# Seven-product input projections in two more blocks, and a modulation product shared by three engines during output projections

## The reference

```python
def modulation(cond, w, b):
    m = jax.nn.silu(cond) @ w + b
    return m.reshape(cond.shape[0], 1, N_MOD, D_MODEL)

def modulate_in(x, g_pre, mod, j):
    return rmsnorm(x, g_pre) * (1.0 + mod[:, :, 3 * j + 1]) + mod[:, :, 3 * j]

def gated_residual(x, out, g_post, mod, j, weight):
    return x + weight * mod[:, :, 3 * j + 2] * rmsnorm(out, g_post)

def swiglu(h, w13, w2):
    a, g = jnp.split(h @ w13, 2, axis=-1)
    return (jax.nn.silu(g) * a) @ w2
```

## Time and profile before

| | us |
|---|---|
| median of 3 runs | 2538.57 (2536.57 to 2541.32) |
| the profiled execution's own time | 2541.83 |
| its span, first to last instruction | 2540.0 |
| PE busy | 2476.5 (97%) |
| DVE busy | 1581.6 (62%) |
| ACT busy | 764.9 (30%) |
| POOL busy | 224.6 (9%) |

### The profile page before, as it was taken

One profiled execution on the slowest core, in us unless ns is written; L12 is line 12 of the kernel. 1 busy time (PEld: TensorE's weight loads), 2 busy tenths in 40 slices (PEclk: granted clock), 3 DMA queues, 4 the chain that ended last, 5 costly groups with the idle time before them and its releaser, 6 DMA issues. The chain is left out here.

```text
span 2540.0 us, 40285 instructions
## 1 busy us (share of the span) xinstructions
PE 2476.5 (97%) x15180; PEld 2295.7 (90%) x15180; DVE 1581.6 (62%) x2779; ACT 764.9 (30%) x1418; POOL 224.6 (9%) x299
## 2 busy tenths in 40 slices
PE   6999999999998899999999999999999999999998
PEld 5998999799888789989988998899799979989997
DVE  4887588734554678738875885233454458845864
ACT  4111111333444441111124211111331153523432
POOL 0000000201114210000002000000110011201211
PEclk9999999999999999999999999999999999999999
DMA  6554445333223335434551553222312223323332
GB/s 242 160 141 133 133 149 167 107 77 81 48 56 88 88 107 149 134 100 141 149 170 55 150 153 99 80 74 87 96 59 75 87 79 117 83 71 99 88 113 103
DMA packets 385035, 278.64 MB, mean 110 GB/s; under 512 B 39414, under 2 KB 354550, under 8 KB 383894
## 3 DMA queue, kind: packets, MB, share of 16 engines
q1 hardware_dynamic: 384918, 277.06, 36.4%
HBM read 270.04 MB, written 6.94 MB: 109 GB/s over the span
## 5 line engine op out<-in xcount | busy, mean ns | idle before, releaser
L1879 DVE TENSOR_TENSOR w_lo<-w_raw,w_hi 128x1024 fp32r<-128x1024 f32 (+1 forms) x363 | 354.5, 979 | 501.2 <-ACT w_hi L1303 496.8
L1303 ACT ACTIVATE w_hi<-w_raw 128x1024 fp32r<-128x1024 f32 (+1 forms) x363 | 309.2, 854 | 832.4 <-PE psum L921 425.3
L921 PE MATMUL psum<-hT_hi,w_hi 128*128 128x320 f32 x2432 | 554.8, 309 | 4.0 <-DVE w_lo L1879 3.3
L921 PE MATMUL psum<-hT_lo,w_hi 128*128 128x320 f32 x2432 | 554.1, 309 | 0.0
L921 PE MATMUL psum<-hT_hi,w_lo 128*128 128x320 f32 x2432 | 553.8, 309 | 0.0
L921 PEld LDWEIGHTS psum<-hT_hi,w_hi 128*128 128x128 f32 x2432 | 406.3, 188 | 5.7 <-DVE w_lo L1879 2.8
L921 PEld LDWEIGHTS psum<-hT_lo,w_hi 128*128 128x128 f32 x2432 | 406.8, 188 | 0.0
L921 PEld LDWEIGHTS psum<-hT_hi,w_lo 128*128 128x128 f32 x2432 | 406.6, 188 | 0.0
L1848 DVE SCALAR_TENSOR_TENSOR mod_acc<-ada_raw,cond_silu,mod_acc 128x256 f32<-128x256 f32 x896 | 365.4, 479 | 0.0
L848 PE MATMUL psum<-w_hi,act_hi 128*128 128x512 f32 x800 | 318.1, 398 | 4.6 <-DVE w_lo L1879 4.5
L849 PE MATMUL psum<-w_lo,act_hi 128*128 128x512 f32 x800 | 316.3, 395 | 0.0
(11 more groups left out here) (281 smaller groups left out, 3548.1 us busy)
## 6 DMA issues: line engine op xcount, KB each, us to landing
w_raw<-in_ffn_w_dram SPq DMA_DIRECT2D x156, 512.0 KB, 4.1
ada_raw<-in_ada_w_dram SPq DMA_DIRECT2D x128, 512.0 KB, 3.6
w_raw<-in_ffn_w_dram SPq DMA_DIRECT2D x148, 256.0 KB, 2.7
w_raw<-in_ab_w_in_dram SPq DMA_DIRECT2D x28, 512.0 KB, 4.1
w_raw<-in_sc_w_in_dram SPq DMA_DIRECT2D x24, 512.0 KB, 4.0
w_raw_next<-in_ffn_w_dram SPq DMA_DIRECT2D x20, 512.0 KB, 5.2
ada_first<-in_ada_w_dram SPq DMA_DIRECT2D x4, 2048.0 KB, 19.0
held_raw<-in_ffn_w_dram SPq DMA_DIRECT2D x28, 256.0 KB, 3.7
```

Of the source, the lines that this page charges most:

```text
L921: last = mm(IN[p][0:width, h, 0:HT], a, b[:, k, h * HT:(h + 1) * HT], start=(k == 0 and a is hi and b is hT_hi), stop=(k == KD - 1 and a i ...
L1303: A(dst, src, ACT.Copy).then_inc(w_hi_ok, 1)
L1879: V.tensor_tensor(d_, a, b.bitcast(F32), ALU.subtract).then_inc(w_lo_ok, 1)
```

## The change

The third and fourth block take the seven-product form as well, with three plain pairs in the first half. The jobs of these blocks go (`JOBS` keeps block 0). Layer 1's modulation is now made in nine *sums* of 1024 columns (`MODS`): three in the first output stage of block 2 and one in its second, the same in block 3, and the ninth in the first output stage of block 5. A sum has 8 *steps*, one per slice k. A step loads a tile `ada_tile` of 128 x 1024 (512 KB, three slots). VectorE multiplies and adds the first 576 columns for both conditions, as before; of the other 448 ScalarE makes the two scaled copies (one to `mod_scaled`, one over the tile), and GpSimd adds them to its accumulators. After 8 steps TensorE sums over the partitions with a column of ones (`pick`), 8 matmuls of 288 or 224 columns on four column groups (`modulation`). VectorE adds the bias (`modulation_rows`) and SyncE stores the rows. The steps of a first output stage stand at units 1 to 17 (24 steps; block 5's eight at the same pace, at units 1 to 5), those of a second at units 2 to 9 (8 steps). The output stages use other PSUM banks, and the x rows that were loaded back evenly in the second output stage are, but for the first, now loaded after its last weight.

Core of the diff. `load_mods` runs on SyncE behind the load of unit u's weight, `modulation` on TensorE behind output unit u, `scale_step` on ScalarE, the first `add_step` on GpSimd and the second on VectorE:

```diff
-PLAIN = {5: (3, 0)}
+PLAIN = {2: (3, 0), 3: (3, 0), 5: (3, 0)}
...
-JOBS = {0: (0, 2 * D, (HF, HF), (3, 3)), 2: (1, 0, (HF, HF), (1, 1)), 3: (1, 6 * D, (HF, 0), (1, 0))}
+JOBS = {0: (0, 2 * D, (HF, HF), (3, 3))}
+MODS = {2: ([(1, 0), (1, D), (1, 2 * D)], [(1, 3 * D)]), 3: ([(1, 4 * D), (1, 5 * D), (1, 6 * D)], [(1, 7 * D)]), 5: ([(1, 8 * D)], [])}
+GROUPS = (288, 288, 224, 224)
+ON_DVE, MODC = 576, 1024
+SUM_AT = lambda ph, z: STEP_AT(ph["half"], len(ph["mods"]))[8 * z + 7] + (2 if ph["half"] == 0 else 0)
+STEP_AT = lambda half, n: [1 + j * 17 // 24 for j in range(8 * n)] if not half else [2 + j for j in range(8 * n)]
...
+            def load_mods(ph, u):
+                n = len(ph["mods"])
+                at_u = STEP_AT(ph["half"], n)
+                for j in range(8 * n):
+                    if (2 if j < 3 else at_u[j - 3] + 3) != u:
+                        continue
+                    g = 8 * ph["mb"] + j
+                    if j == 0:
+                        load_bias_rows(ph, 0)
+                        sp.wait_ge(pe_prod, SEVEN * ph["g1"])
+                    if j >= 3:
+                        sp.wait_ge(ada_used[0], USED(g - 3))
+                        sp.wait_ge(ada_used[1], USED(g - 3))
+                    layer, col = ph["mods"][j // 8]
+                    slot, count = TILE(g)
+                    src = ada_w[layer].rearrange("(p k) n -> p k n", k=KD)[:, j % 8, col:col + MODC]
+                    dma(ada_tile[ph["half"]][slot][:], src).then_inc(ada_landed[slot], 16)
...
+            def modulation(ph, u):
+                    pe.wait_ge(ada_used[0], USED(8 * b + 7))
+                    pe.wait_ge(ada_used[1], USED(8 * b + 7))
...
+                    for cd in range(2):
+                        for i in range(4):
+                            acc, c = (ACC_D(ph, z), G_AT[i]) if i < 2 else (ACC_P(ph, z), G_AT[i] - ON_DVE)
+                            last = mm(PS[32 * i:32 * i + 2, bank, 0:GROUPS[i]], pick[:, 1 - cd:3 - cd], acc[:, cd, c:c + GROUPS[i]], start=(cd == 0), stop=(cd == 1))
+                    last.then_inc(mod_mm, 1)
...
+            def scale_step(ph, j):
+                act.wait_ge(ada_landed[slot], count)
...
+                tile = ada_tile[h][slot][:, ON_DVE:MODC]
...
+                if k > 2:
+                    act.wait_ge(ada_used[1], USED(g - 2))
+                A(scaled[h][:, k % 2, :], tile, ACT.Copy, scale=csil[:, 0, k:k + 1])
+                A(tile, tile, ACT.Copy, scale=csil[:, 1, k:k + 1]).then_inc(mod_scaled, 1)
...
+            def add_step(ph, j):
...
+                pool.wait_ge(mod_scaled, g + 1)
+                pool.wait_ge(ada_used[1], USED(g - 1))
+                for cd, src in enumerate((scaled[h][:, k % 2, :], ada_tile[h][TILE(g)[0]][:, ON_DVE:MODC])):
+                    acc = ACC_P(ph, j // 8)[:, cd, :]
+                    pool.tensor_tensor(acc, acc, src, ALU.add).then_inc(ada_used[1], 1)
...
+            def add_step(ph, j):
+                dve.wait_ge(ada_landed[slot], count)
...
+                    if k == 0:
+                        V.tensor_scalar(acc, w, col, None, ALU.mult).then_inc(ada_used[0], 1)
+                    else:
+                        V.scalar_tensor_tensor(acc, w, col, acc, ALU.mult, ALU.add).then_inc(ada_used[0], 1)
```

More of the change, by code:

```diff
@@ L1031, in out_phase @@
                     last.then_inc(pe_unit, 1)
+                    if seven(ph):
+                        modulation(ph, u)
                 if not held:
@@ L1410, in out_splits @@
                             split_held(s, ph, i)
+                    if seven(ph):
+                        for j, at_u in enumerate(STEP_AT(ph["half"], len(ph["mods"]))):
+                            if at_u == u:
+                                scale_step(ph, j)
                 if final:
@@ L1756, in _ @@
                             pool.tensor_tensor(S2[:], S1[:], A11(g), ALU.subtract).then_inc(ws_ok, 1)
+                        for j in range(8 * len(ph["mods"])):
+                            add_step(ph, j)
                 if kind == "sc":
@@ L2034, in out_phase @@
                             split_held(s, ph, i)
+                    if seven(ph):
+                        for z in range(len(ph["mods"])):
+                            if min(SUM_AT(ph, z) + 3, len(units) - 1) == u:
+                                modulation_rows(ph, z)
+                        for j, at_u in enumerate(STEP_AT(ph["half"], len(ph["mods"]))):
+                            if at_u == u:
+                                add_step(ph, j)
                     z, r = divmod(u - 1 - LATE[ph["half"]] if late else u, 3)
-                    sooner = 2 if late and not final else 0
+                    sooner = 2 if (late or seven(ph)) and not final else 0
                     if sooner and u == K + 1:
```

209 lines of the change are left out of this document (172 added, 37 removed).

## The result

The changed kernel takes **2586.85 us**, the median of four runs (2584.41 to 2592.79), against 2538.94 for the kernel before (four runs now, one more than in the table ahead of the prediction): a ratio of **1.019**, 95% interval 1.017 to 1.021, so 48 us slower. The forecast was 2553, the range 2487 to 2582. The direction was right, the loss more than three times as large as forecast, and the time lies outside the range. Repeated runs of one kernel lie up to 10 us apart, so a difference of a few us against a kernel that ran once is not told from none.

What follows compares the result with a forecast made beforehand. TensorE, busy 97% of the span, was taken to bound the kernel. Terms -62.6 - 1 + 52.2 + 17.8 + 8.4 = +14.8 us on the profiled 2541.8 gave 2556.6, so a median of 2553 us; range 2487 to 2582.

Steps and rivals of the forecast that it cites:

- Part 1 and 2: Blocks three and four: the seven-product form saves 62.6 us; taking jobs out of the input stages saves 1 us.
- Part 3: The nine sums over partitions on TensorE, 8 small fp32 matmuls each: 1.1 us per sum.
- Part 4, the price of a turn: First output stages: VectorE and GpSimd take turns, so one addition and one VectorE step together cost 1.63 us.
- GpSimd's end: First output stage: GpSimd's chain of additions ends at 93.8 us, 88.8 plus 5 for tiles that land late.
- Part 4, the step that failed: First output stage: unit 18's split comes at 89.3 us, 4.5 before GpSimd's end; stage ends at 104.4, +26.1 each.
- evacuations on the path: Copies of finished banks out of PSUM delaying TensorE: +8, allowed only within the forecast's own range.
- its case's own range: Spread of the forecast's main case, which had chance 0.68: 2530 to 2573 us.
- Part 5 and 6: Eight steps in each second output stage, +8.9 each or +17.8; ninth sum in the sixth block's first output stage, +8.4.
- rival 2: VectorE and GpSimd exclude each other for whole instructions: 1.86 us per pair, +29.0, 2582 us; chance 0.10.
- Rival 1: VectorE's and GpSimd's steps run side by side without turns, making the kernel faster: 2491 us; chance 0.18.
- Rival 3: TensorE's clock drops in first output stages, units taking 7.0 us instead of 5: +24, 2577 us; chance 0.04.

Runs made afterwards that it cites:

- no_mods: Changed kernel with the nine modulation sums left out, blocks reading the first layer's modulation instead: 2482.82 us, 0.979 to the kernel before.
- no_reload: Experiment 4: changed kernel, each stage loading only its first three ada_w tiles and reusing them, all arithmetic kept (sums wrong): 2582.8 us, one run.
- evac_first: Changed kernel, VectorE copying four finished PSUM banks before its unit 12 steps in blocks three and four's first output stages: 2585.8 us, 1.018 to the kernel before.
- no_adds_evac_first: Changed kernel without GpSimd's 126 additions (sums wrong) and with the PSUM copies ahead of VectorE's unit 12 steps: 2517.7 us.
- no_adds: Changed kernel without GpSimd's 126 additions (sums wrong), scalings, tile loads and VectorE's steps kept: 2536.2 us.
- one_input: Changed kernel with VectorE's multiply-add of the sums replaced by a plain multiply with one tensor input (sums wrong): 2564.3 us.

## Why the prediction was wrong

- **Part 1 and 2**, -63.6: right in mechanism, somewhat too large: no_mods measured -57.9 (spans) or -53.8 (medians). The two first halves gave 12.4 and 11.9 there and not 13.8.
- **Part 3**, 1.1 us per sum: units with a sum take 4.67 and the next 3.62 instead of 3.51, so 1.3. Right.
- **Part 4, the price of a turn**, 1.63 per pair: 1.61, 1.55, 1.63 read. Right. GpSimd's end (93.8 against 94.8) is near in part by luck: 2.9 us too much for the chain without late tiles, 3.9 too little for late tiles (experiment 4).
- **Part 4, the step that failed:** "ScalarE's split of unit 18 stands behind its last scaling and that behind GpSimd's last step but two ... 89.3". It lets the path to TensorE leave GpSimd's chain 4.5 us before that chain's end and hangs the weight on ScalarE. But the last half of the split is VectorE's, and it stands in VectorE's queue behind VectorE's own last step. In after ScalarE was through with unit 18 at 91.9 and VectorE at 93.8, 4.5 later than forecast; in no_reload, where no tile is late, at 85.4 and 89.2 (84.3 forecast). VectorE's list was only checked without turns (33.7 us of steps, splits at 0.60), and taken to fit. With turns it is the bound: in no_reload it takes 84.0 us without a gap, 42 multiply-adds at 1.36, 17 splits at 1.20, and the copies and row additions, 6.8, that were in no sum. From the split of unit 18, four units and the third sum end at 109.1; from that of unit 17 (90.7), five units and the sum end at 109.6.
- The other 2.7 to 3.2 us of that stage: TensorE left unit 11 late because of the copies and never waited again, ending at 112.3. The forecast had "evacuations on the path" as +8 in its case's own range and no place for it; evac_first shows that they are worth 2.1 and 0.1 us in the two stages, nothing clear of noise in the time, and no_adds_evac_first that they are worth 18.5 us once the additions are gone.
- **Part 5 and 6**, +21.6 and +8.4: +28.3 and +10.7. In the second output stages TensorE began unit 10 at 47.8 and 47.7 us where 45.8 was forecast, and among the held weights, at the first transposition of the next block's x (behind VectorE's normed row, line 2102), it was held up 1.9 and 1.6 us longer than in no_mods. In the sixth block it began unit 6 at 31.4 (29.7 forecast). no_adds, with 88.8 and 87.5 us for the second stages and 82.7 for the sixth block's, puts 7.6, 8.5 and 6.3 us down to the additions; no_reload (96.6, 95.4, 89.5) puts nothing down to late tiles there.
- **Rivals.** The time lies near that of rival 2 (2582), but its mechanism, 1.86 per pair, did not occur; reading the total as its proof would be wrong. Rival 1 was wrong. Rival 3's clock did fall, to 0.91 on average in the two first stages: in the third block's 0.87 up to unit 12, 0.81 in unit 12, which takes 4.3 us instead of 3.51, and 1.00 behind it. So where TensorE alone sets the pace it cost 0.8 us of that stage. Up to unit 12 TensorE is idle 21.7 of 73.9 us, most of it waiting for VectorE; how much of the slower clock reached the end through those waits was not separated by a run.

## What to carry to other kernels

When two engines take turns, sum the list of each of them with the turns in it, every split, copy and row addition included, and see which is longer; a chain followed along one of them misses the other. Then ask what stands behind the last item of that list. Here it was the split of a weight, and behind that TensorE had four units and a sum left to do. And check the alternative of not sharing: the same work on VectorE alone was 34 us cheaper than the shared one with early copies (2551.4 against 2585.8), on TensorE in batches of three tiles 55 us (2530.9).

## What was not expected of the hardware

- VectorE's 576-column plain multiply with one tensor input, 0.52 us alone, took 1.39 beside GpSimd's addition (one_input).
- A pair of one VectorE multiply-add (0.81 alone) and one GpSimd addition (1.16 alone) takes 1.6 us, neither 1.16 nor 1.97.
- Small fp32 matmuls dropped into a stream of others cost TensorE 0.28 us for each interruption beside 0.49 us for four of 224 and 288 columns on four column groups, and each of them leaves two records in the trace.
